# Routed experts in pieces of 32 rows instead of 64, two sub-turns to a step, on one Trainium2 core

## What is computed

```python
def _moe_ffn(h, w_router, b_router, w_e1, w_e3, w_e2, w_s1, w_s3, w_s2):
    aff = jax.nn.sigmoid((h @ w_router).astype(jnp.float32))
    _, eidx = lax.top_k(aff + b_router, TOP_K_EXPERTS)          # 6 of 64 experts per row
    gsel = jnp.take_along_axis(aff, eidx, axis=-1)
    gates = gsel / jnp.sum(gsel, -1, keepdims=True) * ROUTED_SCALE
    ...                                                          # rows sorted by expert
    def expert_block(args):
        tok, e = args
        return _swiglu(h_pad[tok], w_e1[e], w_e3[e], w_e2[e])    # (silu(x w1) * (x w3)) w2
    ...
    routed = jax.ops.segment_sum(y, slot_tok, num_segments=n_tok + 1)[:n_tok]
    return routed + _swiglu(h, w_s1, w_s3, w_s2)
```

## Time and profile before

| | us |
|---|---|
| median of 3 runs | 2426.61 (2419.96 to 2429.17) |
| profiled execution, its own time | 2424.11 |
| its span (first to last instruction) | 2422.3 |
| expert phase in the trace | about 1467 to 2358 |
| PE busy (matmuls) | 1979.4, 82% of the span |
| up-products of the experts, L3127 | 498.1 busy, 38.4 idle before them |
| down-products, L3169 | 252.1 busy, 1.3 idle before them |
| DVE, ACT, POOL busy | 907.4, 594.7, 448.9 |

### The profile page before, as it was taken

The page is one execution under the profiler, slowest core; times in us unless marked ns, Lnnn a source line. Parts: engine busy times, 40 slices in busy tenths (PEclk is TensorE's granted clock), DMA queues, the critical chain, the costliest instruction groups (busy, mean ns, idle before and its releaser), DMA issues. The chain is left out here.

```text
span 2422.3 us, 29647 instructions
## 1 busy us (share of the span) xinstructions
PE 1979.4 (82%) x9088; PEld 1075.4 (44%) x9089; DVE 907.4 (37%) x2006; ACT 594.7 (25%) x1185; POOL 448.9 (19%) x745
## 2 busy tenths in 40 slices
PE   5699934974368868958998977999999999999965
PEld 1466624542136655525775643444333443333322
DVE  6100064849898553316545731111111111111107
ACT  2100001226657832223111111111111111111114
POOL 0000040034401100100532001222222222222210
PEclk8899966886557988978997998999999999999987
DMA  9700020010000015550243158879889889998867
GB/s 362 263 0 1 1 55 3 3 34 27 18 1 1 1 40 240 213 217 24 87 165 118 44 217 309 286 247 307 275 311 320 285 264 310 327 353 305 267 207 284
DMA packets 89760, 411.30 MB, mean 170 GB/s; under 512 B 21481, under 2 KB 28393, under 8 KB 60362
## 3 DMA queue, kind: packets, MB, share of 16 engines
q1 hardware_dynamic: 62594, 296.24, 32.0%
q0 software_dynamic: 25856, 109.60, 16.5%
q10 hardware_dynamic: 1232, 4.46, 0.5%
HBM read 355.41 MB, written 63.95 MB: 173 GB/s over the span
## 5 line engine op out<-in xcount | busy, mean ns | idle before, releaser
L3127 PE MATMUL psum<-wx,hT_x 128*64 128x512 f32 x2208 | 498.1, 603 | 38.4 <-DMA wx<-in_w_e 26.4
L3127 PEld LDWEIGHTS psum<-wx,hT_x 128*64 128x64 f32 x2208 | 184.5, 139 | 351.5 <-issue 351.5
L3053 DVE COPY hT_x<-psum 128x512 f32<-128x512 f32 x69 | 47.7, 692 | 562.8 <-PE psum L3114 562.8
L3169 PE MATMUL psum<-wx,hidT_x 128*64 128x512 f32 x1104 | 252.1, 598 | 1.3 <-ACT hidT_x L3070 1.3
L3070 ACT COPY hidT_x<-psum 128x256 f32<-128x256 f32 x69 | 25.7, 373 | 497.9 <-PE psum L3153 497.9
L2424 PE MATMUL psum<-wx 128*128 128x512 f32 (+1 forms) x288 | 131.0, 615 | 1.4 <-PEq L2102 1.4
L3169 PEld LDWEIGHTS psum<-wx,hidT_x 128*64 128x64 f32 x1104 | 73.1, 136 | 128.0 <-issue 118.2
L3104 DVE TENSOR_SCALAR y_x<-psum,slot_gate 128x512 f32<-128x512 f32 x69 | 51.8, 751 | 194.9 <-PE psum L3169 192.1
L3043 POOL DMA_INDIRECT scr_acc<-y_x,add_idx x69 | 110.6, 1602 | 32.3 <-issue 32.3
L2424 PEld LDWEIGHTS psum<-wx 128*128 128x128 f32 (+1 forms) x288 | 84.5, 296 | 43.5 <-issue 16.7
L3077 ACT ACTIVATE y_x<-psum,slot_gate 128x512 f32<-128x512 f32 x69 | 47.5, 689 | 222.3 <-PE psum L3169 219.0
(11 more groups left out here) (693 smaller groups left out, 3143.7 us busy)
## 6 DMA issues: line engine op xcount, KB each, us to landing
wx<-in_w_e SPq DMA_DIRECT2D x201, 1024.0 KB, 9.8
wa<-in_w_ada SPq DMA_DIRECT2D x8, 3072.0 KB, 12.8
xt<-in_x_prompt SPq DMA_DIRECT2D x16, 512.0 KB, 4.9
f<-scr_acc SPq DMA_DIRECT2D x16, 512.0 KB, 9.9
scr_acc<-zero SPq DMA_DIRECT2D x11, 512.0 KB, 16.4
wx<-in_w_out SPq DMA_DIRECT2D x2, 2048.0 KB, 12.9
scr_x<-x POOLq DMA_DIRECT2D x8, 512.0 KB, 3.1
scr_h<-h POOLq DMA_DIRECT2D x8, 512.0 KB, 3.8
```

Source lines behind the costliest of these rows:

```text
L3127: mm = pe.matmul(psum[at, 2 + par, :].rearrange("p (j f) -> p j f", j=2), hT[:, par, k, at], w13[:, :, k], start=(k == 0), stop=(k == KD - 1))
L3169: mm = pe.matmul(psum[at, 5 + c, :], hidT[:, k, at], w2[:, k, c * 512:(c + 1) * 512], start=(k == 0), stop=(k == 1))
```

## The change

SUB becomes 32, and there are four accumulators ("copies") instead of two. A step still holds 128 rows and two trios' slots are used in it: it covers two sub-turns, s = 0 and 1, of two experts each, 32 rows for each expert. To fill the 128 columns of the array with groups of 32, each expert's up-product is cut in two halves, the even and the odd columns of w1 and w3 (`half:FE:2`): the four column groups are two experts by two halves. So `up` is called twice for a step, with 32 matmuls of 256 columns each in the program (16 of 512 before in one call). `up(b+1, ..., 0)` stands where the up-product stood; `up(b+1, ..., 1)` comes at the end of the body, behind the down-product, which has 16 matmuls of 512 columns in four groups of 32 (8 in two groups of 64 before). Each `up` reads its own two table values.

```diff
-SUB = 64
-LANES, QUEUES = P // SUB, 6
+SUB, COPIES = 32, 4
+LANES, QUEUES = 2, 6
-TURNS = -(-(TOK * TOPE // SUB + EXPERTS) // QUEUES)
-STEPS = TURNS * TRIOS
+TURNS = -(-(TOK * TOPE // SUB + EXPERTS) // (4 * QUEUES)) * 4
+SUBS = TURNS * TRIOS
+STEPS = SUBS // 2
@@ out_phase, SyncE: zero fill
-            for i in range(ACC // P):
-                sp.dma_start(scr["acc"][ACC + i * P:ACC + (i + 1) * P], zero[:]).then_inc(z_out, 16)
+            for i in range(ACC // P, COPIES * ACC // P):
+                sp.dma_start(scr["acc"][i * P:(i + 1) * P], zero[:]).then_inc(z_out, 16)
@@ expert_phase, SyncE
-                        free = load(sp, T_FREE + rank, LANES, 2 * STEPS)
+                        up_free = load(sp, T_UP_FREE + rank, COPIES, 4 * SUBS + 8)
+                        dn_free = load(sp, T_DN_FREE + rank, COPIES, 4 * STEPS + 8)
                         sp.wait_ge(w_land[m], 32 * turn)
-                        sp.wait_ge(up_ps, free)
+                        sp.wait_ge(up_ps, up_free)
                         fetch_up(sp, a, wx, e, q, w_land[m])
                         sp.wait_ge(w2_land[m], 16 * turn)
-                        sp.wait_ge(dn_ps, free)
+                        sp.wait_ge(dn_ps, dn_free)
                         fetch_down(sp, a, wx, e, q, w2_land[m])
@@ expert_phase, TensorE
-            def up(b, trio, par):
-                even = load(pe, T_LAND + b, 16, 16 * FETCHES)
-                odd = load(pe, T_LAND + STEPS + b, 16, 16 * FETCHES)
+            def up(b, j, par, s):
+                even = load(pe, T_LAND + 2 * b + s, 16, 16 * FETCHES)
+                odd = load(pe, T_LAND + SUBS + 2 * b + s, 16, 16 * FETCHES)
                 pe.wait_ge(w_land[0], 2 * even)
                 pe.wait_ge(w_land[1], 2 * odd)
...
-                        mm = pe.matmul(psum[at, 2 + par, :].rearrange("p (j f) -> p j f", j=2), hT[:, par, k, at],
-                                       w13[:, :, k], start=(k == 0), stop=(k == KD - 1))
+                        for half in range(2):
+                            mm = pe.matmul(psum[lane(l, half), 2 + par, s * FE:(s + 1) * FE].rearrange(
+                                "p (j f) -> p j f", j=2), hT[:, par, k, lane(s, l)], w13[:, :, k, half:FE:2],
+                                start=(k == 0), stop=(k == KD - 1))
...
             def body(b, j, turn, n):
                 par = j % 2
-                even = load(pe, T_LAND + b, 16, 16 * FETCHES)
-                odd = load(pe, T_LAND + STEPS + b, 16, 16 * FETCHES)
+                even = load(pe, T_LAND + 2 * b + 1, 16, 16 * FETCHES)
+                odd = load(pe, T_LAND + SUBS + 2 * b + 1, 16, 16 * FETCHES)
                 with pe.If(b + 1 < n):
-                    up(b + 1, (j + 1) % TRIOS, 1 - par)
+                    up(b + 1, (j + 1) % UNROLL, 1 - par, 0)
...
                 for c in range(2):
                     for k in range(2):
-                        for l, at in enumerate(lanes):
...
+                        for s in range(2):
+                            for l in range(LANES):
...
+                                mm = pe.matmul(psum[lane(s, l), 5 + c, :], hidT[:, s, lane(l, k)],
+                                               w2[:, k, c * 512:(c + 1) * 512], start=(k == 0), stop=(k == 1))
...
+                with pe.If(b + 1 < n):
+                    up(b + 1, (j + 1) % UNROLL, 1 - par, 1)
@@ final_phase
-                for l in range(LANES):
-                    at = l * ACC + i * P
-                    sp.dma_start(f[l][0:n, i], scr["acc"][at:at + n]).then_inc(f_land[i], 16)
+                if i >= RING:
+                    sp.wait_ge(summed, i - RING + 1)
+                for copy in range(COPIES):
+                    at = copy * ACC + i * P
+                    sp.dma_start(f[copy * SUB:(copy + 1) * SUB, i % RING, 0:n // SUB],
+                                 scr["acc"][at:at + n].rearrange("(q t) d -> t q d", t=SUB)).then_inc(f_land[i], 16)
...
-                    for l in range(LANES):
-                        mm = pe.matmul(psum[0:n, 2 * (i % 4) + c, :], cst["ident"][0:n, 0:n],
-                                       f[l][0:n, i, c * 512:(c + 1) * 512], start=(l == 0), stop=(l == LANES - 1))
+                    for q in range(n // SUB):
+                        mm = pe.matmul(psum[q * SUB:(q + 1) * SUB, 2 * (i % 4) + c, :], stack[:],
+                                       f[:, i % RING, q, c * 512:(c + 1) * 512], start=True, stop=True)
```

More of the change, by code:

```diff
@@ L2682, in _ @@
+            for c in range(COLS):
                 nc.vector.tensor_copy(want[:, c, 1:2], queue[:])
[L2683 removed]
+                nc.vector.tensor_scalar(want[:, c, 3:4], turn[:, c:c + 1], 2.0 * TRIOS, float(4 - 2 * TRIOS),
                                         ALU.mult, ALU.add)
             for p in range(1, TRIOS):
[L2686 to L2688 removed]
@@ L2754, in _ @@
             seq(nc.vector.scalar_tensor_tensor(sub[:, 0:1], run[:], length[:], turn[:, 0:1], ALU.mult, ALU.add))
-            seq(nc.vector.tensor_scalar(sub[:, 1:2], sub[:, 0:1], float(SPLIT // QUEUES), None, ALU.add))
-            for c in range(2):
+            for c in range(1, COLS):
+                last = nc.vector.tensor_scalar(sub[:, c:c + 1], sub[:, 0:1], float(c * SPLIT // QUEUES), None, ALU.add)
+            seq(last)
+            for c in range(COLS):
                 at = sub[:, c:c + 1]
@@ L2896, in _ @@
                     one_col = cst["ones"][0:SPLIT]
-                    pe.matmul(psum[:, 7, 0:2], cst["before"][0:SPLIT], change[0:SPLIT], start=True, stop=False)
-                    pe.matmul(psum[:, 7, 1:2], one_col, change[0:SPLIT, 0:1], start=False, stop=True)
-                    pe.matmul(psum[0:1, 7, 8:8 + STEPS], change[0:SPLIT, 0:1], seen[0:SPLIT, 0],
-                              start=True, stop=False)
-                    pe.matmul(psum[0:1, 7, 8:8 + STEPS], change[0:SPLIT, 1:2], seen[0:SPLIT, 1],
-                              start=False, stop=True).then_inc(rank_ps, 1)
+                    pe.matmul(psum[:, 7, 0:COLS], cst["before"][0:SPLIT], change[0:SPLIT], start=True, stop=False)
+                    for c in range(1, COLS):
+                        for d in range(c):
+                            pe.matmul(psum[:, 7, c:c + 1], one_col, change[0:SPLIT, d:d + 1],
+                                      start=False, stop=(c == COLS - 1 and d == c - 1))
+                    for c in range(COLS):
+                        mm = pe.matmul(psum[0:1, 7, 8:8 + SUBS], change[0:SPLIT, c:c + 1], seen[0:SPLIT, c],
+                                       start=(c == 0), stop=(c == COLS - 1))
+                    mm.then_inc(rank_ps, 1)
                 if i == 5:
                     pe.wait_ge(pick_made, 1)
-                    for v in range(3):
-                        for c in range(2):
-                            mm = pe.matmul(psum[0:1, 7, P + v * FETCHES:P + (v + 1) * FETCHES],
+                    for v in range(WANTS):
+                        for c in range(COLS):
+                            mm = pe.matmul(psum[0:1, 7, PICK + v * FETCHES:PICK + (v + 1) * FETCHES],
                                            want[0:SPLIT, c, v:v + 1], picked[0:SPLIT, c],
-                                           start=(c == 0), stop=(c == 1))
+                                           start=(c == 0), stop=(c == COLS - 1))
                     mm.then_inc(pick_ps, 1)
@@ L3078, in body @@
                                      scale=r["slot_gate"][:, bass.ds(b, 1)]).then_inc(y_act, 1)
+                with act.If(b + 1 < n):
+                    silu_of(1 - par, b + 2)
             blocks(act, body)
@@ L3166, in body @@
                     for k in range(2):
-                        for l, at in enumerate(lanes):
-                            w2 = wx[:, LANES * (j % TRIOS) + l, 2 * KD * FE:].rearrange("p (k n) -> p k n", k=2)
-                            mm = pe.matmul(psum[at, 5 + c, :], hidT[:, k, at], w2[:, k, c * 512:(c + 1) * 512],
-                                           start=(k == 0), stop=(k == 1))
-                            if c == k == 1:
-                                mm.then_inc(dn_ps, 1)
+                        for s in range(2):
+                            for l in range(LANES):
+                                w2 = wx[:, LANES * ((2 * j + s) % TRIOS) + l, 2 * KD * FE:].rearrange(
+                                    "p (k n) -> p k n", k=2)
+                                mm = pe.matmul(psum[lane(s, l), 5 + c, :], hidT[:, s, lane(l, k)],
+                                               w2[:, k, c * 512:(c + 1) * 512], start=(k == 0), stop=(k == 1))
+                                if c == k == 1:
+                                    mm.then_inc(dn_ps, 1)
+                with pe.If(b + 1 < n):
+                    up(b + 1, (j + 1) % UNROLL, 1 - par, 1)
             blocks(pe, body)
@@ L3283, in _ @@
             nc.vector.memset(eps[:], EPS)
+            for copy in range(COPIES):
```

(6 more changed lines are left out.)

157 lines of the change are left out of this document (90 added, 67 removed).

## The result

The changed kernel takes 2869.01 us (median of four runs, 2863.87 to 2870.67), the kernel before 2423.99 on the same chip: a ratio of 1.1829, 95% interval 1.1808 to 1.1850. The direction was forecast, the size was not: +445 us against +234, and the time lies above the range. The profiled execution has a span of 2867.1 us against 2422.3.

What follows compares the result with a forecast made beforehand. PE itself was taken to set the expert phase's pace. Terms -110 + 162 + 64 + 90 + 10 + 12 + 3 + 3 = +234 on 2424.1 gave 2658, forecast as 2660 us; range 2440 to 2800.

Steps and rivals of the forecast that it cites:

- Nine steps fewer: Expert phase: 60 steps instead of 69, at 12.22 us each, claimed to save 110 us.
- The bare chain: PE's branches and table reads before each first half: 2.85 us uncovered, step 14.92 us, +162 us over 60 steps.
- The clock: First halves of up-products: granted clock falls after the idle gap in 5 of 7 cases, +64 us (0 to 94).
- The weights: Expert phase: 16 first halves wait for up-weights fetched behind a held w2, +90 us (+18 to +132).
- Loop code: PE's larger loop body may be fetched again: 1 us at each of ten turns, +10 us (0 to 38).
- The final phase: Final tiles load 2.6 MB instead of 1.6, at 411 GB/s: +12 us (0 to +65 at half rate).
- Zero fill and route: 20 more zero-fill DMAs, +3 us (0 to 10), and small DVE route-table operations, +3 us (0 to 10).
- half rate: Rival: up-products run at half rate through the column stride or a lower clock, 2950 us; chance 0.11.
- the chain stays hidden: Rival: PE's lead is longer for small matmuls, so branches and reads stay covered, step 12.32 us, 2494 us; chance 0.19.

## Why the prediction was wrong

The mechanisms were named, but for the empty steps, and each was shown by an edit that takes it away. What failed is the sum: the chain, the final phase and the weights came out 40 to 46 us too low each, another 41 us stood in no term, and the range was narrower than the bounds written beside the terms.

- **Nine steps fewer, -110**: right, 60 steps.
- **The bare chain, +162**: the place and the cause are right; measured +208. A step at full clock is 15.75 us and not 14.92. Of the 0.83 between them 0.60 is the gap, 3.45 and not 2.85, and 0.36 the second half, 3.82 and not 3.46; 0.09 is in the first half, and behind the down-product 0.22 less was spent than forecast. The lead of 38 instructions and the number of reads were right; that a read costs 0.75 us as in the earlier trace rows was not, and the stride, costed at nothing, adds 0.18 to each half.
- **The clock, +64**: measured +95. "5 of 7" was taken from seven gaps of the kernel before; after the change 57 of 59 first halves were slow.
- **The weights, +90**: 16 places, as walked through; measured 133 for them instead of 117, +130 with the start and less what was there. In these places the first half started 14.5 to 16.0 us behind the down-product instead of 13.9.
- **Loop code, +10**: the size was left between 0 and 38. Measured +28 at the turn of the loop, and +41 that no term held: the 12 jumps over empty steps behind the last one. I counted turns of the loop and left out its empty steps, which the kernel before passes at 0.2 us each; here they take 2.9 to 5.1 us each, with 23 instruction packets arriving around them. The rule of the Trainium skill that the prediction quoted ("Runtime: NRT & Kernel Launch", "Instruction fetch mechanics") speaks of any taken branch whose target lies outside the two pages of instructions held just then. The trace agrees with it as far as these jumps are taken branches and instructions were fetched there. It does not show so small a window: the loop of before, some 880 instructions, jumps back in 0.22 us, and the earlier trace rows have no instruction packets.
- **The final phase, +12**: measured +54, the term that failed by most for its size. The loads into 32 partitions run at 228 GB/s, not at the 411 of the earlier trace rows. The half rate stood in the text as the upper bound of +65, and I took the other end: the row of 411 was of 128-partition loads, and nothing in the trace spoke for that rate at 32.
- **Zero fill and route, +6**: +4.

By terms above the forecast: 46 chain, 42 final phase, 41 empty steps, 40 weights, 31 clock, 18 turn of the loop, less 6 outside the steps of the expert phase and 2 for zero fill and route: 210, of the 211 by which the time missed the sum.

The range failed in its own arithmetic. The bounds held for each term but the empty steps and, by 1 us, the clock. But the text says that all terms at their high end give about 2780, and the bounds beside the terms add up to +460, or 2887 (2845 with the weights left at +90, since their bound supposes that there is no gap). So the measured time lay within the bounds and outside the range made of them. The rival "half rate" of up-products was wrong (3.82 at full clock), "the chain stays hidden" too.

## What to carry to other kernels

When matmuls are cut smaller, look first at what the engine's sequencer does between them. Its lead was some 38 instructions here both before and after the change, so smaller matmuls cover less of the same branches and reads (1.5 us of a chain of 4.8, before the change 3.6 of 3.8), and the idle gap is then paid twice, by the clock of what follows. A loop whose instructions are fetched again in every turn (97 packets here) pays at its taken jumps, also at the jumps over steps that are empty: 0.2 us each with three steps written out, 3 to 5 with six. Where a row gives a rate, carry its shape along with it: 411 GB/s of 128-partition loads said nothing of 32 partitions. And when the range is set, add up the bounds that stand beside the terms.

## What was not expected of the hardware

- Jumps on PE's sequencer: 208 to 233 ns with three steps of the changed kernel written out, 208 to 248 with six of the kernel before, 2.9 to 5.4 us with six steps of the changed kernel.
- Loads from device memory into 32 partitions moved 228 GB/s, into 128 partitions 418, the same bytes and queue.
- Table reads on PE's sequencer took 0.4 to 1.4 us beside GpSimd's issue of a gather and 0.30 elsewhere; that the gather is the cause is not shown.
- A moving operand with a stride of 8 bytes took 3.82 us where one without took 3.64, 5% more.
